# In seven norms of a two-block network, VectorE writes each chunk's low part one scaled chunk after it instead of two

## The reference, cut to what matters

```python
def rms_norm(x, gain):
    xf = x.astype(jnp.float32)
    y = xf * lax.rsqrt(jnp.mean(xf * xf, axis=-1, keepdims=True) + NORM_EPS)
    return (y * gain.astype(jnp.float32)).astype(x.dtype)

def modulate(x, shift, scale):
    return x * (1 + scale[:, None, :]) + shift[:, None, :]
...
        u = modulate(rms_norm(h, norm_ffn[layer]), sh2, sc2)
        h = h + g2[:, None, :] * swiglu(u, ffn_w_in[layer], ffn_w_out[layer])
```

## Time and profile before

| what | us |
|---|---|
| median of 3 runs | 2433.08 (2431.8 to 2437.09) |
| the profiled execution, its own time | 2433.55 |
| its span in the trace | 2431.5 |
| TensorE matmul busy | 2220.8 |
| VectorE busy | 1408.7 |
| ScalarE busy | 765.2 |
| GpSimd busy | 419.3 |

### The profile page before, as it was taken

The page is one execution under the profiler, slowest core; times in us unless marked ns, Lnnn a source line. Parts: engine busy times, 40 slices in busy tenths (PEclk is TensorE's granted clock), DMA queues, the critical chain, the costliest instruction groups (busy, mean ns, idle before and its releaser), DMA issues.

```text
span 2431.5 us, 25733 instructions
## 1 busy us (share of the span) xinstructions
PE 2220.8 (91%) x10088; PEld 1769.6 (73%) x10088; DVE 1408.7 (58%) x1918; ACT 765.2 (31%) x977; POOL 419.3 (17%) x272
## 2 busy tenths in 40 slices
PE   7899999989999979999899999698797886999996
PEld 5688788767888868666788888476486664888885
DVE  5676676446767773575544444753545546556556
ACT  1443333332222232465322222443133233322221
POOL 0000000079888833010000000002300000000000
PEclk9899999989999989999999999799899887999998
DMA  6343231235555524221223232121022321332320
GB/s 253 115 156 104 91 123 49 86 121 190 182 192 181 175 102 156 96 79 36 84 90 104 87 104 96 45 100 57 0 87 90 100 70 35 104 104 89 102 87 35
DMA packets 39647, 252.68 MB, mean 104 GB/s; under 512 B 4563, under 2 KB 4755, under 8 KB 11048
## 3 DMA queue, kind: packets, MB, share of 16 engines
q1 hardware_dynamic: 33176, 234.11, 27.7%
q0 software_dynamic: 3008, 10.63, 1.4%
q10 hardware_dynamic: 3344, 6.29, 0.7%
HBM read 244.73 MB, written 6.29 MB: 103 GB/s over the span
## 4 chain that ended last, share of the span: by engine, by line
PE 81%; DVE 10%; issue 4%; POOL 2%; ACT 2%; DMA 1%; SPq 0%; ACTq 0%; DVEq 0%; POOLq 0%
PE bank L656 23%; PE bank L657 23%; PE bank L658 23%; PE bank L869 2%; DVE w_lo L1643 1%; PE bank L703 1%; DVE scr L1673 1%; PE bank L785 1%; PE bank L987 1%; PE bank L779 1%; PE bank L997 1%; PE bank L1008 1%; POOL raw L572 1%; PE bank L1100 1%; DVE scr L1711 1%
## 5 line engine op out<-in xcount | busy, mean ns | idle before, releaser
L656 PE MATMUL bank<-u_hi,w_hi 128*128 128x512 f32 x1740 | 704.8, 405 | 48.9 <-DVE u_lo L1705 11.2
L657 PE MATMUL bank<-u_lo,w_hi 128*128 128x512 f32 x1740 | 688.3, 396 | 0.0
L658 PE MATMUL bank<-u_hi,w_lo 128*128 128x512 f32 x1740 | 687.8, 395 | 0.0
L1643 DVE TENSOR_TENSOR w_lo<-raw,w_hi 128x2048 fp32r<-128x2048 f32 x165 | 432.9, 2624 | 286.0 <-ACT w_hi L1194 285.9
L656 PEld LDWEIGHTS bank<-u_hi,w_hi 128*128 128x128 f32 x1740 | 333.9, 192 | 140.3 <-issue 57.5
L1194 ACT ACTIVATE w_hi<-raw 128x2048 fp32r<-128x2048 f32 x165 | 314.9, 1909 | 342.2 <-PE bank L658 308.0
L658 PEld LDWEIGHTS bank<-u_hi,w_lo 128*128 128x128 f32 x1740 | 333.2, 191 | 71.9
L657 PEld LDWEIGHTS bank<-u_lo,w_hi 128*128 128x128 f32 x1740 | 334.0, 192 | 65.4 <-issue 0.2
L656 PE MATMUL bank<-g_hi,w_hi 128*128 128x512 f32 x740 | 294.4, 398 | 24.1 <-DVE w_lo L1643 15.5
L657 PE MATMUL bank<-g_lo,w_hi 128*128 128x512 f32 x740 | 290.8, 393 | 0.0
L658 PE MATMUL bank<-g_hi,w_lo 128*128 128x512 f32 x740 | 290.2, 392 | 0.0
(11 more groups left out here) (251 smaller groups left out, 2265.5 us busy)
## 6 DMA issues: line engine op xcount, KB each, us to landing
raw<-in_wts SPq DMA_DIRECT2D x221, 1024.0 KB, 4.9
spectra<-pool ACTq DMA_DIRECT2D x16, 256.0 KB, 2.0
scr<-in_rel POOLq DMA_DIRECT2D x16, 256.0 KB, 3.2
pool<-spectra POOLq DMA_DIRECT2D x16, 256.0 KB, 3.0
H<-in_x ACTq DMA_DIRECT2D x1, 2048.0 KB, 20.7
out<-H SPq DMA_DIRECT2D x1, 2048.0 KB, 7.5
pool<-in_window POOLq DMA_DIRECT2D x1, 1024.0 KB, 8.5
pool<-in_filt_w POOLq DMA_DIRECT2D x1, 512.0 KB, 5.9
```

Of the source, the lines that this page charges most:

```text
L656: pe.matmul(out, lh, rh, start=start, stop=False, skip_group_check=True)
L657: pe.matmul(out, lh, rl, start=False, stop=False, skip_group_check=True)
L658: return pe.matmul(out, ll, rh, start=False, stop=stop, skip_group_check=True)
L1643: dve.tensor_tensor(w_lo[w % hi_ring][:, :], raw[W_STREAM[w] % raw_ring][:, :], w_hi[w % hi_ring][:, :].bitcast(F32), ALU.subtract).then_i ...
```

## The change

L(c) is issued after S(c + 1) instead of after S(c + 2). Before, VectorE's order was S0 S1 S2 L0 S3 L1 S4 L2 S5 L3 S6 L4 S7 L5 L6 L7; now it is S0 S1 L0 S2 L1 S3 L2 S4 L3 S5 L4 S6 L5 S7 L6 L7. The instructions are the same, and so are their waits. No other engine's order is changed.

```diff
@@ -1709,10 +1709,9 @@
                     if c >= 4:
                         dve.wait_ge(u_l, count + c - 3)
                     dve.scalar_tensor_tensor(tn[c % 4], H[:, c, :], gain(c), bank[6][:, :], ALU.mult, ALU.mult).then_inc(u_t, 1)
-                    if c >= 2:
-                        lower(c - 2)
-                lower(6)
-                lower(7)
+                    if c >= 1:
+                        lower(c - 1)
+                lower(KC - 1)
```

## The result

| | before | after |
|---|---|---|
| median | 2433.47 us (20 runs) | 2437.59 us (19 runs) |
| lowest to highest | 2424.6 to 2437.9 | 2434.1 to 2441.1 |
| ratio of the two | | 1.0018 [1.0011, 1.0026] |
| mean granted clock of those runs | 0.9524 | 0.9509 |
| profiled execution, its own time | 2433.55 | 2438.51 |

The forecast was 2433.8, in a range up to 2437.5. The time came out 0.09 us above that range, 3.8 above the forecast. The 0.18% lie within the 0.2% called "same", but the interval reaches beyond it and leaves out zero: the kernel is slower by about 4 us, where 0.75 had been summed. (The mean clock of before is that of the 127 runs beside the experiments; the clock of these 20 is not on record.) One more run of after took 2895.25 us at a mean clock of 0.737; it is in none of these numbers.

The account below looks back on a forecast made before the run. TensorE was taken as the bound, busy 2220.8 of 2431.5 us. The norms' terms, 0.74 + 0.45 + 0.81 - 0.40 - 0.40 - 0.45 + 0 = +0.75 us, on the median 2433.08 gave 2433.8 us, range 2430.2 to 2437.5.

Parts of the forecast that it names:

- same: Outcome class for the whole kernel: time within about 0.2% of before; chance 0.945.
- L(0) and L(7) against A: VectorE in ffn0: first remainder 0.40 us earlier after waiting 0.26 for ScalarE's rounding, last remainder 0.45 later.
- ffn0: Norm where POOL waits for the last remainder and its lock holds w_lo: +0.45 us, bounds 0 and +0.91.
- mix0: Norm whose last rounding comes 0.97 us later against a slack of 0.23: +0.74 us, bounds 0 and +0.97.
- pre2: Norm whose second slot already waits for w_lo, which goes 0.81 us later: +0.8, bounds 0 and +0.9.
- kv: Norm where TensorE's first slot starts earlier and w_lo has slack: -0.40 us, bounds -0.20 and -0.66.
- ffn1: Norm where TensorE starts earlier and the second slot's w_lo still has time: -0.40 us, bounds -0.20 and -0.66.
- mlp_pre2: Norm where TensorE's first slot starts earlier, as in kv: -0.45 us, bounds -0.22 and -0.66.
- mix1: Norm whose first remainder is unchanged; last remainder and w_lo come 0.9 and 1.3 us later, with slack: 0.
- The sum: The terms of all seven norms added: +0.75 us for the whole kernel; the forecast had chance 0.50.
- Rival 2: TensorE's clock falls behind pre2's longer idling, +1.6 us more, +2.35 us in all, 2435.4 us; chance 0.24.
- if the moment of its rise stays where it is: First slots of kv and ffn1: with the clock's rise fixed, starting 0.40 us earlier gains only half; bound -0.20.

Follow-up runs that it names:

- gains: New order only in the norms kv, ffn1 and mlp_pre2, the rest as in the kernel before; ratio 0.9996, in its repeat 1.001.
- costs: New order only in the norms mix0, ffn0 and pre2, the rest as in the kernel before; ratio 1.001.
- pre2only: New order in the norm pre2 alone, the rest as in the kernel before; ratio 1.0023.
- again: The changed kernel (after) run once more, unchanged; ratio to before 1.0018.
- mix1: As a kernel: new order in the norm mix1 alone, the rest as in the kernel before; ratio 1.0009.
- extra4: The kernel before with the first matmul of pre2's second slot repeated 4 times, a pure delay; ratio 1.0016.
- best: gains with pre2's second w_hi put ahead of its norm on ScalarE, old order elsewhere; ratio to before 1.0013.

## Why the prediction was right, and where it was wrong

- **L(0) and L(7) against A.** Right: L(0) 0.39 us nearer to S(0) in ffn0, where 0.40 was worked out, with an idle time of 0.18 (0.26). w_hi was +0.94 (0.91).
- **ffn0, mix0, pre2, kv, ffn1, mlp_pre2, mix1.** Right to within 0.05: second slots +0.49, +0.75 and +0.81, first slots -0.39, -0.39 and -0.44, mix1 none. In time, the two sets of gains average -0.4 ± 0.35 at equal clock, not the -1.25 (-0.7 ± 0.45 against the runs of before of their own sets). That is nearer to the lower bound of 0.62 (half of each, if the clock's rise stays where it is). In pre2 the rise did stay: 8.04 us behind the spreading matmul in before and in after, though the slot started 0.43 earlier in after. In the profiled gains, ffn1's rise moved with the start (8.59 and 8.20). So this term is bounded, not settled.
- **The sum.** +0.75 against +1.35 ± 0.4 and +0.85 ± 0.5 at equal clock. As a fixed cost it was right.
- **Rival 2**, a fall of the clock behind pre2's 2.45 us. It is undecided as a thing that sometimes happens: there is no fall there in the profiles of after, costs and pre2only, but one in again, and one behind the old 1.94 us in mix1. Its size of +1.6 us for a fall was right, as the windows show (7 matmuls). It is not the account of the 3 us: extra4 and best have a lower mean clock without the longer gap.
- **The failed step** is the treatment of the clock as something local. The prediction bounded it norm by norm ("if the moment of its rise stays where it is") and priced it at one gap. It had no term for a change of the mean clock over the whole program, and that term measured 0.0015 of mean clock, 3.0 us by the slope, four times the whole sum. In the profiled execution the loss shows as 4.6 us between mix1 and ffn1, at no gap that the prediction priced. What should have raised the question stood there: the earlier trace rows have 0.98, 1.00 and 0.50 within one program, and TensorE is 91% busy, so that most of what its clock loses goes into the time.
- **The range** took the spread of the three runs (-1.3 to +4.0) as noise about a time that the sum would move. In 127 runs of before the spread is the clock's: executions at a mean clock of 0.956 to 0.957 took 2424.1 to 2429.8 us, those at 0.949 to 0.950 took 2437.0 to 2442.3. If a change can move the mean of that distribution, the range must reach by a few us to either side of the sum. 2437.5 was too near, and the chance of 0.04 for slower by over 0.2% was too small.

What stays open: why the versions with pre2's change or delay have a lower mean clock over many executions, while the profiled ones lost their time ahead of it; whether mix0's delay costs 0.7 or nearer 1.7; and whether 1.8 us of shift is really cheaper than 0.9. The runs show these differences. They don't give their cause, nor a rule by which a shift could be chosen.

## What to carry over

When a schedule change moves less than the kernel's own spread, measure the mean granted clock of every run and compare at equal clock: that recovers the fixed cost to about half a microsecond, and tells it from what the clock added. Read TensorE's busy time first, because more busy time for the same number of matmuls is clock and not waiting. To learn whether an edit's cost is its own or its shift's, put a pure delay of the same length in the kernel before, at the same place. Then find in the trace where the time was lost: here it was lost ahead of the edit, in a part that is the same in both programs, and so the explanation that suggested itself has no support from it. And keep no reordering for a gain of 1 us where the mean clock differs from version to version by 3 to 4.

## What the runs showed of the hardware

- The time of this kernel follows the mean granted clock with about -1940 us for 1.0. An estimate for a program that was TensorE's work alone is 2431.5 / 0.952 = 2554; that the slope is smaller fits a program in which some time passes in waits for other engines.
- The Trainium skill ("TensorE: Matmul & The Clock Gate", section "Part 1: The HAM clock gate (the "warmup" mystery)") says that the default is the throttled state, which activity releases, and that for modelling the ramp costs less than 1% of a typical span. The first agrees with the rows of 0.76 to 0.77 and 0.63 behind the norms ffn0, kv, ffn1, pre2 and mlp_pre2; behind mix0, whose first slot starts at 0.47, the clock was full. The second speaks of one ramp, and this program has many: the mean clock of before is 4.8% below full, by the slope above an estimated 93 us or 3.8% of the span, and its differences from run to run make most of the 19 us between the fastest and the slowest of before.
- Idle time alone did not decide where the clock fell: pre2's 2.45 us were followed by full clock in after and its 2.43 us by the lower level in again, the 2.5 us ahead of mix1's scores by full clock in before and costs and by the lower level in after, pre2only and extra4, 2.58 us by the lower level in ffn1, and 0.73 and 1.06 us with 16 small matmuls between them by either, in before and in after.
